# Expert blocks with gate and up ahead of down, six 1 MB weight buffers, compressor tiles between projections

## The reference, cut to what matters

```python
for l in range(DEPTH):                       # DEPTH = 2
    m = token_mixer(x, w_in[l], ...)         # attention, short convolution, retention, merged
    x = layer_norm(ALPHA * x + m, ...)
    if l % 2 == 0: f = swiglu(x, ffn_gate, ffn_up, ffn_down)
    else:          f = moe_swiglu(x, ...)    # top 2 of 8 experts, each (silu(x@g) * (x@u)) @ d, D_FF = 3584
    x = layer_norm(ALPHA * x + f, ...)
# in the mixer's attention: keys and values of blocks of 32 tokens at stride 16, compressed by an MLP
hid = gelu(flat @ w1 + b1);  k_cmp, v_cmp = hid @ w2 + b2
```

## Time and profile before

| | us |
|---|---|
| median of three runs | 1907.62 (1906.16 to 1909.39) |
| the profiled execution, whole | 1904.11 |
| its span, first to last instruction | 1902.3 |
| PE busy / DVE / ACT in the span | 1853.1 / 1432.6 / 1133.7 |
| DMA, share of the 16 engines over the span | 0.71 (0.93 in the experts) |

### The profile page before, as it was taken

The page is one execution under the profiler, slowest core; times in us unless marked ns, Lnnn a source line. Parts: engine busy times, 40 slices in busy tenths (PEclk is TensorE's granted clock), DMA queues, the critical chain, the costliest instruction groups (busy, mean ns, idle before and its releaser), DMA issues.

```text
span 1902.3 us, 28024 instructions
## 1 busy us (share of the span) xinstructions
PE 1853.1 (97%) x11100; PEld 1613.4 (85%) x11104; DVE 1432.6 (75%) x1212; ACT 1133.7 (60%) x972; POOL 0.2 (0%) x4
## 2 busy tenths in 40 slices
PE   7999999999999999999999999999999999999996
PEld 6899998999978999996888888888888887888885
DVE  4685577544466665768889889888898888888987
ACT  5444444343436444445777777777677777777774
POOL 0000000000000000000000000000000000000000
PEclk9999999999999999999999999999999999999998
DMA  7633444554436333454998989989989899899993
GB/s 313 230 144 133 156 177 178 188 187 176 181 144 251 134 139 139 171 206 160 369 364 325 369 335 356 381 323 368 362 333 369 328 361 352 328 365 357 347 362 151
DMA packets 36026, 504.69 MB, mean 265 GB/s; under 512 B 3968, under 2 KB 4096, under 8 KB 5248
## 3 DMA queue, kind: packets, MB, share of 16 engines
q1 hardware_dynamic: 34960, 498.07, 69.5%
q10 hardware_dynamic: 1008, 5.77, 0.8%
HBM read 502.78 MB, written 1.05 MB: 265 GB/s over the span
## 4 chain that ended last, share of the span: by engine, by line
PE 79%; DVE 7%; DMA 7%; ACT 4%; issue 3%; SPq 0%; DVEq 0%; ACTq 0%
PE PS L345 14%; PE PS L347 13%; PE PS L346 13%; PE PS L331 11%; PE PS L333 10%; PE PS L332 10%; DMA raw<-wstream 7%; DVE w_lo L1117 4%; ACT w_hi L828 3%; PE PS L715 1%; PE PS L741 1%; PE PS L483 1%; PE PS L515 1%; PE PS L498 1%; PE PS L784 0%
## 5 line engine op out<-in xcount | busy, mean ns | idle before, releaser
L1117 DVE TENSOR_TENSOR w_lo<-raw,w_hi 128x2048 fp32r<-128x2048 f32 x472 | 1077.1, 2290 | 322.7 <-ACT w_hi L828 320.8
L828 ACT ACTIVATE w_hi<-raw 128x2048 fp32r<-128x2048 f32 x472 | 901.9, 1915 | 343.7 <-PE PS L347 181.2
L331 PE MATMUL PS<-xT_hi,w_hi 128*128 128x256 f32 x1456 | 419.1, 288 | 7.0 <-DVE w_lo L1117 6.1
L332 PE MATMUL PS<-xT_lo,w_hi 128*128 128x256 f32 x1456 | 412.3, 283 | 0.0
L333 PE MATMUL PS<-xT_hi,w_lo 128*128 128x256 f32 x1456 | 412.2, 283 | 0.0
L345 PE MATMUL PS<-w_hi,xT_hi 128*128 128x512 f32 x896 | 355.1, 396 | 2.6 <-DVE xT_lo L1556 1.5
L347 PE MATMUL PS<-w_hi,xT_lo 128*128 128x512 f32 x896 | 349.6, 390 | 0.0
L346 PE MATMUL PS<-w_lo,xT_hi 128*128 128x512 f32 x896 | 349.0, 390 | 0.0
L331 PEld LDWEIGHTS PS<-xT_hi,w_hi 128*128 128x128 f32 x1456 | 279.5, 192 | 18.8 <-issue 14.5
L332 PEld LDWEIGHTS PS<-xT_lo,w_hi 128*128 128x128 f32 x1456 | 279.7, 192 | 0.2
L333 PEld LDWEIGHTS PS<-xT_hi,w_lo 128*128 128x128 f32 x1456 | 279.5, 192 | 0.0
(11 more groups left out here) (246 smaller groups left out, 1326.6 us busy)
## 6 DMA issues: line engine op xcount, KB each, us to landing
raw<-wstream SPq DMA_DIRECT2D x236, 2048.0 KB, 8.8
soft<-ln ACTq DMA_DIRECT2D x4, 1024.0 KB, 6.3
X<-x SPq DMA_DIRECT2D x1, 1024.0 KB, 4.9
out<-X ACTq DMA_DIRECT2D x2, 512.0 KB, 2.7
cst<-consts SPq DMA_DIRECT2D x1, 906.0 KB, 11.0
sm<-small SPq DMA_DIRECT2D x1, 729.0 KB, 12.7
bufA<-router ACTq DMA_DIRECT2D x1, 512.0 KB, 3.4
rg<-constb SPq DMA_DIRECT2D x1, 335.0 KB, 11.4
```

Source lines behind the costliest of these rows:

```text
L331: mm(o, wh, rhs_hi[:, k, :], start=(k == 0), stop=False)
L332: mm(o, wh, rhs_lo[:, k, :], start=False, stop=False)
L828: activate(w_hi[:, at % RING], raw_half(at // 2 % RING, at % 2), ACT.Copy).then_inc(hi_done, 1)
L1117: v.tensor_tensor(w_lo[:, at % RING], raw_half(at // 2 % RING, at % 2), w_hi[:, at % RING], ALU.subtract).then_inc(lo_done, 1)
```

## The change

Four things are done at once. Nothing is computed differently.

1. `raw` becomes six buffers of one sub (1 MB), loaded again one by one.
2. The mixer's first ten subs come in the order: projection for the compressor, q, compressor, q, compressor, k and v, compressor, k and v, compressor, gates. So each compressor sub stands behind a projection.
3. V and the gates are turned in the middle of sub 10 and no more before sub 11, and ACT copies them at s == 9 behind the first exponentials. The table order on ACT changes: the gates' tanh (s == 9) stands ahead of gelu, which moves from s == 8 to s == 9.
4. In the experts gate and up of block n+1 both come before down of block n. The transposes of block n stand between gate and up.

```diff
-        raw = sb("raw", [P, RING, 2 * SUB])
+        raw = sb("raw", [P, RAW, SUB])
-                sp.wait_ge(lo_done, 2 * index - 2 * RING + 2)
+                sp.wait_ge(lo_done, index - RAW + 1)
+HEAD = {0: 0, 1: 1, 3: 2, 5: 3, 7: 4, 9: 5}
+COMPRESS = (2, 4, 6, 8)
                 def attention_between(s):
                     j, late = divmod(s - STEP0, 2)
+                    if s == STEP0:
+                        values_to_tokens()
 # PE, experts
                 def body(n, s, at, item=None):
-                    first = item is not None
-                    up(s, at)
-                    if first:
-                        slots_to_tokens(item)
-                    pe.wait_ge(esilu_rdy, n + 1)
-                    up_half(s + 2, at + 2, 0, 0)
+                    pe.wait_ge(esilu_rdy, n + 1)
+                    up_half(s, at, 0, 0)
+                    up_half(s + 1, at + 1, 0, 1)
+                    if item is not None:
+                        slots_to_tokens(item)
                     hidden_transposes(n)
-                    up_half(s + 3, at + 3, 0, 1)
+                    up_half(s + 2, at + 2, 1, 0)
+                    up_half(s + 3, at + 3, 1, 1)
                     down(n, s + 4, at + 4, ...)
 # PE, last block of an item
-                    up(s0 + (FFN - 4), MOE0 + 2)
-                    gather(i + 1, range(DK // 2))
                     hidden_transposes(n)
-                    gather(i + 1, range(DK // 2, DK))
+                    gather(i + 1)
                     down(n, s0 + (FFN - 2), MOE0 + 4, False, True)
 # ACT, experts: start of an item, then the body
-                    split(MOE0 - 1 + RING, i * NB)
-                    split(MOE0 + RING, i * NB)
-                    split(MOE0 + 1 + RING, i * NB)
-                    silu_block(i * NB, s0 + 1)
+                    split(MOE0 + 2, i * NB)
+                    split(MOE0 + 3, i * NB)
+                    silu_block(i * NB, s0 + 1)
+                    split(MOE0 + 4, i * NB)
+                    split(MOE0 + 5, i * NB)
                         if c == 2:
+                            act.wait_ge(ehid_rdy, n + 1)
+                            silu_block(n + 1, s + 1)
                             ...
                             hidden_block(n)
-                        split(MOE0 + 2 + c + RING, k)
-                        if c == 3:
-                            silu_block(n + 1, s + c)
+                        split(MOE0 + 6 + c, k)
 # DVE, experts: start of an item, then the body
-                    split(MOE0 - 1 + RING, i * NB)
-                    split(MOE0 + RING, i * NB)
+                    split(MOE0 + 2, i * NB)
+                    split(MOE0 + 3, i * NB)
+                    split(MOE0 + 4, i * NB)
                     add_scattered(i, (0, 1))
-                    split(MOE0 + 1 + RING, i * NB)
+                    split(MOE0 + 5, i * NB)
+                    hidden_block(i * NB, s0 + 3)
-                        if c == 1:
-                            hidden_block(n, s + 1)
+                        if c == 1 and item is not None:
+                            add_scattered(item, (2, 3))
                         if c == 2:
                             lower(n)
-                        if c == 3 and item is not None:
-                            add_scattered(item, (2, 3))
-                        split(MOE0 + 2 + c + RING, k)
+                        if c == 4:
+                            hidden_block(n + 1, s + 3)
+                        split(MOE0 + 6 + c, k)
```

More of the change, by code:

```diff
@@ L60 @@
 RING = 3
+RAW = 6
 NEXT = (0, MIX, LAYER, MOE0)
-NTILES = (MOE0 + NE * FFN) // 2
-ITEM_TILES = FFN // 2
+NSUBS = MOE0 + NE * FFN
 PA = (0, 1)
@@ L263, in trunk @@
         act_chain, dve_chain = sem("act_chain"), sem("dve_chain")
[L265 to L271, removed]
         block = ctx.enter_context(nc.Block())
@@ L285, in _, with load @@
                     sp.dma_start(sm[:, :, :], small.rearrange("l p c -> p l c")).then_inc(const_in, 16)
-            rest = NTILES - RING
-            def tile(slot, src, index):
-                sp.wait_ge(lo_done, 2 * index - 2 * RING + 2)
+            rest = NSUBS - RAW
+            def load(slot, src, index):
+                sp.wait_ge(lo_done, index - RAW + 1)
                 sp.dma_start(raw[:, slot], src).then_inc(landed[slot], 16)
[L293 to L298, removed]
+            with sp.Fori(0, rest // RAW) as i:
+                for c in range(RAW):
+                    t = i * RAW + (RAW + c)
+                    load(c, wstream[bass.ds(t, 1)].rearrange("a p c -> (a p) c"), t)
+            for t in range(RAW + rest // RAW * RAW, NSUBS):
+                load(t % RAW, wstream[t], t)
             sp.wait_ge(table_rdy, 1)
@@ L304, in _ @@
                     e = sp.value_load(table[0:1, bass.ds(i, 1)], min_val=0, max_val=NE - 1)
[L305 to L311, removed]
+                    with sp.Fori(0, FFN // RAW) as b:
+                        for c in range(RAW):
+                            t = e * FFN + b * RAW + (MOE0 + c)
+                            load((NSUBS + c) % RAW, wstream[bass.ds(t, 1)].rearrange("a p c -> (a p) c"),
+                                 i * FFN + b * RAW + (NSUBS + c))
+            for c in range(2):
+                load((NSUBS + c) % RAW, wstream[c], extra * FFN + (NSUBS + c))
         @block.tensor
@@ L859, in after @@
                     sub = OUT0 > s >= BRANCH0
-                    if not (s in (0, 1, 2, 3, 7, 9, 10, 11, 15, 20, 21, 22, 23) or sub):
+                    if not (s in (0, 1, 3, 5, 8, 9, 10, 11, 15, 20, 21, 22, 23) or sub):
                         return
                     act.wait_ge(hi_done, base + s + RING)
-                    act.wait_ge(sub_used, base + s + 1)
[L864 to L871, removed]
+                    if s == 0:
+                        for kv in range(2):
+                            last = activate(z[:, 0, kv, 2].rearrange("p r q -> p q r"),
+                                            sm[:, l, S_POS + kv * P:S_POS + (kv + 1) * P].rearrange(
+                                                "p (q r) -> p q r", r=8), ACT.Copy)
+                        last.then_inc(z_hi_rdy, 1)
+                    act.wait_ge(sub_used, base + s + 1)
+                    if s in (1, 3):
+                        c = s - 1
+                        activate(qT[:, c:c + 2], pa(HEAD[s]), ACT.Copy).then_inc(act_free, 1)
+                    elif s == 0:
                         for g in range(NG):
                             for par in range(2):
[L874 to L878, removed]
+                                activate(z[par * DH:(par + 1) * DH, 0, :, g].rearrange("p v r q -> p v q r"),
+                                         pa(0)[g * DH:(g + 1) * DH, :, par::2].rearrange("p v (q r) -> p v q r", r=8),
+                                         ACT.Copy).then_inc(z_hi_rdy, 1)
+                    elif s == 5:
                         for g in range(NG):
@@ L963, in mixer @@
                         act.dma_start(wr, router).then_inc(wr_in, 16)
-                    if s == 8:
+                    if s == 9:
                         after_hidden()
[L966 to L971, removed]
                     if STEP0 - 1 <= s <= STEP0 + 2 * NS:
@@ L980, in mixer @@
                             exps(j)
+                    if s == STEP0 - 1:
+                        act.wait_ge(vt_ps, l + 1)
+                        activate(gate[:, :, :].rearrange("p t c -> p (t c)"), PS[:, TB, 0:TT * 24], ACT.Copy,
+                                 bias=0.5, scale=0.5)
+                        activate(V[:, :, :, :].rearrange("p a t c -> p (a t c)"), PS[:, TB + 1, :],
+                                 ACT.Copy).then_inc(v_rdy, 1)
                     if s in (22, 24):
@@ L1664, in host_layout @@
         first = list(cut(np.concatenate([q, kv, ngp], 1), DK))
-        subs += first[:4]
+        compress = []
         for kv_ in range(2):
@@ L1668, in host_layout @@
             for h in range(2):
-                subs.append(w1[8 * h:8 * h + 8].transpose(1, 0, 2).reshape(P, SUB))
-        subs += first[4:]
+                compress.append(w1[8 * h:8 * h + 8].transpose(1, 0, 2).reshape(P, SUB))
+        subs += [first[2], first[0], compress[0], first[1], compress[1], first[3], compress[2], first[4], compress[3],
+                 first[5]]
         subs += list(cut(np.concatenate([conv_c, conv_h, conv_b, ret], 1), DK))
@@ L1688, in host_layout @@
                 subs += [d[2 * b], d[2 * b + 1]]
-    head = np.stack(subs).reshape(-1, 2, P, SUB).transpose(0, 2, 1, 3).reshape(-1, P, 2 * SUB)
-    stream = np.empty((NTILES, P, 2 * SUB), np.float32)
-    stream[:len(head)] = head
-    assert len(head) == MOE0 // 2
-    t = len(head)
+    assert len(subs) == MOE0
+    stream = np.empty((NSUBS, P, SUB), np.float32)
+    stream[:MOE0] = subs
+    t = MOE0
     def wide(w):
-        return rows(w, DK).reshape(P, DK, NB, 512).transpose(2, 0, 1, 3).reshape(NB, P, 2 * SUB)
```

(19 more changed lines are left out.)

85 lines of the change are left out of this document (40 added, 45 removed).

## The result

The changed kernel takes **1883.1 us** (median of four runs, 1882.98 to 1883.21) against 1906.9 for the kernel before (1902.2 to 1909.4 in four runs here, 1902 to 1910 in all runs of this study). The ratio is 0.9876, with a 95% interval of 0.9860 to 0.9891. The forecast was 1892.7 with a range from 1884 to 1902: the direction was right and the size was not. The profiled run of the changed kernel takes 1883.12, span 1881.3.

The account below looks back on a forecast made before the run. PE, busy 97% of the span, was taken as the bound, leaving only its waits to gain. 1904.1 - 8.2 (mixers) - 0.3 (start) - 6.4 (experts) = 1889.2, plus 3.5 to the median: 1892.7 us, range 1884 to 1902.

Parts of the forecast that it names:

- The 3.5 us by which before's median lay above its profiled run: Whole kernel: 3.5 us added to the profiled-run sum of 1889.2 to give a median of 1892.7.
- The charge of 0.8 to 1.1 us a mixer for changes of shape: Mixer: four compressor visits instead of one, each costing PE about 0.27 us there and back.
- the new wait: Experts, item start: PE waits for DVE's splits, 0.46 us at sub 5, 0.37 at sub 7; +1.0 an item with restarts.
- `down`'s wait: Experts, steady blocks: PE's wait for the low half of down's input, 6.1 us listed over ten times, goes through the new order.
- The item without waits: Experts: PE's necessary work in one item, 123.3 us, plus 0.1 for odd changes of operand.
- The two leads: Experts: time from a tile's request to its first use, about 9.7 us before and about 12.4 with six buffers.
- Rival A: Experts give nothing because tiles still land late and the wait moves to `w_lo`: 1899 us, chance 0.22.
- C: Half-size transfers feed the experts too slowly, DMA share above 0.97 with ACT waiting: slower, 1915 to 1961 us, chance 0.06.
- The heads: Mixer: 5.2 us of PE waits removed, net 4.1 a mixer, 8.2 for two, bounds 3 and 5.2 each.
- The checks of slack: Mixer: `z` and sub 3's split ready in time, 0.6 us left; V turned earlier; a possible table load costs 0 to 0.3.
- B: Experts give all: the new wait is hidden, items take 123.4 us, total 1884 us; chance 0.13.
- D: Mixer heads fall short through late `z` copies or the gates' table load, half of 8.2 goes: 1897 us, chance 0.10.

Follow-up runs that it names:

- e1: The kernel before with only the new mixer sub order and V's turn, buffers and experts as before: 1896.05 us.
- e2: The kernel before with only the six buffers of 1 MB: 1891.23 us.
- e4: The changed kernel with the first two adds of the scattered result moved ahead of the split of sub 4 on DVE: 1877.14 us.
- e6: The kernel before with only the six 1 MB buffers, but SP asks for two subs at once, each its own transfer: 1892.96 us.
- e5: The changed kernel without its new order of the experts (new mixer heads and six buffers kept): 1881.29 us.
- e8: The changed kernel with the first adds ahead of sub 4's split and each sub loaded in two 0.5 MB transfers: 1877.03 us.
- e9: The changed kernel without its new experts order, with the second two adds of an item's first block one split later on DVE: 1877.35 us.
- e7: The kernel before with new mixer heads, new experts order and first adds ahead of sub 4's split, tiles still 2 MB: 1878.25 us.

## Why the prediction was wrong, point by point

The forecast was 1892.7 and 1883.1 was measured, 9.6 us less. Three terms of the sum were mis-sized. The 3.5 us by which before's median lay above its profiled run were added to the changed kernel, where that difference is 0.0. The charge of 0.8 to 1.1 us a mixer for changes of shape, which no row shows, is not there (e1: 5.0 us a mixer for 4.1). An item was put at 124.4 us and takes 124.13, and the first item lacks the new wait (3.3 us over eight items). Behind the size stands a step of the mechanism that failed as well: `down`'s wait was credited to the new order alone, and the buffers were put at nothing in the experts, where alone they remove it (e2).

- **The new wait at an item's start** was forecast operation by operation, and stands. DVE's late split: 10.05 us after the first gate forecast, 10.07 measured (1003.56 less 993.49, the first gate, 5.44 ahead of the scatter at 998.93); end of the split behind the adds 15.8, measured 15.88; PE late by 0.46, measured 0.51. At sub 7 I said 0.37 late, and it is 0.07 and the restart (1015.45 to 1015.75 where 0.23 is normal): the split ends at 22.2 as forecast, but PE asks for it at 22.19 and not at 21.86. In all 1.0 against 0.9 (e4). So DVE's and ACT's ends, added up from rows of the kernel before, came out within a tenth of a us; the place of PE at sub 7 was 0.3 off.
- **The item without waits** was put at 123.3 + 0.1. It is 123.2 (e4). Together with the last point that makes 124.4 against 124.13, 0.27 us for each of eight items, 2.2 of the 3.3 us missed here. The rest: the first item has no such wait (998.93 - 875.76 = 123.2), and I charged it 1.0. The rows and the account of PE's work gave the gain as a difference, 125.2 less 124.4, so that the shorter last interval of both kernels doesn't enter.
- **Which edit removes down's wait.** I gave it to the order and took the buffers for a help. Buffers alone give 14.8 us, the order alone 9.7, and both with the heads 1.8 less than buffers and heads. My own reading had the cause: ACT's copy stands behind a split that waits for a tile. What failed was the next step, to price that cause: the buffers stand in the sum at 0.3 us for the start and at nothing in the experts. With both in place the experts gain 9.7 us between the first and the last scatter, less than with the buffers alone (12.0), because the new order brings its own wait. I should have asked what an item costs when the tile is on time, and the answer was in the rows' spread: the shortest item of before took 124.2, already 1.0 below the mean.
- **Why the tiles came late.** The two leads were right as numbers: from SP's issue to ACT's first use the traces have 9.8 us before and 12.4 after (medians), for 9.7 and 12.4. But the longer lead, which I took for what the buffers give, is not needed, as e6 shows. The data are there sooner when they come in smaller pieces: the tile of 2 MB lands 9.4 us after its issue, a sub of 1 MB 6.5, a pair of subs in e6 7.3. I had looked at the lead alone and not at the landing time.
- **A reading that was wrong.** Rival A has a block of 16.8 us fed at 354 GB/s. That is the rate over a whole item (44.0 MB in 124.4 us); the six subs of a block are 6.29 MB, so 374 GB/s. The changed kernel has 370 GB/s and a DMA share of 0.98 between 1030 and 1110 us. That is above the 0.97 that I named as a sign of C, and ACT waits for no tile there. A stood closer than its reasons said, and still did not happen.
- **The heads.** 5.0 each for 4.1. All the waits that I listed went, in both layers. The charge of 0.8 to 1.1 for changes of shape was not there: between a projection and a compressor sub PE goes on at 0.12 us. I had taken it from places where PE changes to other operands after a wait or a transposed tile. 1.8 us of the miss; 0.3 more is the start, where the buffers gave 0.6 for 0.3. The checks of slack (`z`, sub 3, V's turn, the possible extra table load) all held: no wait appeared, and ACT has 973 instructions against 972, the extra load.
- **From the profiled execution to the median.** I added the 3.5 us by which the median of before lay above its profiled run. The changed kernel's median is its profiled run. The runs of before differ by 8 us, those of the changed kernel by 0.2. Late tiles that differ from run to run are the likely reason, for the runs without them (e2, e4, e5, e6, e8, e9) lie within 0.5 to 2.0 us; but e7, with 46 waits for tiles, lies within 1.1, and no trace of a slow run of before was taken, so it is not shown. A sum that removes the waits of one profiled run ends at that run's time, 1889.2, and nothing was to be added. 2.8 to 3.5 us, the largest single term.
- **The rivals.** The time of B (1884) came about, but not by its mechanism: the new wait was not hidden (items take 124.13 us and not B's 123.4), and what brought the time there were the heads, the first item and the median. A and D did not happen. C was tried with twice its number of transfers and cost no time.

In sum 3.5 (median, which stood at 1907.6 then), 3.3 (experts), 2.1 (heads and start), 0.7 (end) make the 9.6 us. The 0.7 are not the change's doing.

## What to carry to other kernels

When one engine's queue holds both the splits of arriving data and the short copies that another engine waits for, a late transfer shows up as a wait for the copy. Before reordering the queue, try whether smaller transfers of the same bytes are in time: here that cost nothing, and gave more than the reordering as first written (14.8 against 9.7 us). After any reordering walk the in-order queues once more for holes; moving two adds by one place was worth 6 us in the changed kernel and 3.9 in e5. And where runs of the kernel before scatter, don't carry the distance from its profiled run to its median over to the new kernel.

## What the runs showed of the hardware

Between 0.5 and 2 MB a transfer the same amount was delivered: 356 or 357 GB/s between 900 and 1850 us in every kernel without listed waits of PE for late tiles (352 in the kernel before). The landing times and the share of the 16 engines differ: medians of 9.4 us for 2 MB (e7, share 0.94), 5.3 to 6.8 for 1 MB (0.91 to 0.93, over e2, e4, e5, e6, e9 and the changed kernel) and 6.0 for 0.5 MB (e8, 0.96). Halving the transfer from 1 to 0.5 MB brought nothing.

PE's granted clock is 1.00 all through the experts. At the very end PE waits 2.2 us for the last rest in both kernels. After it, in the kernel before, the matmuls of the final scatter start 0.34, 0.40 and then 0.43 us apart, where 0.23 is normal:

```profile
1885.02 0.52 PE L784 MATMUL PS<-act_hi 128*128 128x512 f32 x1 [2.21 <-DVE act_lo L1597]
1885.36 0.60 PE L785 MATMUL PS<-act_lo,act_hi 128*128 128x512 f32 x1
1885.76 0.63 PE L784 MATMUL PS<-act_hi 128*128 128x512 f32 x1
1886.19 0.63 PE L785 MATMUL PS<-act_lo,act_hi 128*128 128x512 f32 x1
```

The granted clock there is 1.00 up to 1885 us and 0.50 from 1885.5 to 1887, which are the two levels of 2.4 and 1.2 GHz: it falls 0.35 us after the scatter's first matmul. In the changed kernel the wait is the same (1864.77, 2.21 us idle), the clock is 1.00 up to 1866 us and falls 1.5 us after the first matmul, and most of the scatter still runs at the high level. That is most of the 0.7 us of the stage table's third row. It is luck and not a gain: e4, whose end is written the same, has 17.3 us from the first matmul of its last scatter to the end (1857.98 to 1875.28), as the kernel before, and there the clock has fallen before that matmul. What sets the moment of the fall is not shown. Also open is why the runs of e2, e5 and e9, whose items all take the same time, still differ by 1.5 to 2 us.
